# Projection units with the left 256 tokens through all chunks first, then the right 256, in one bank

## The reference

```python
# layer 1: differential attention beside a sparse attention with compressed tokens
x = x + rms_norm(hybrid_mixer(rms_norm(x, ...), ...), attn_post_norm)
x = x + rms_norm((silu(h @ w_gate) * (h @ w_up)) @ w_down, ffn_post_norm)
# layer 2: short convolution beside forgetting attention ("fox"), then SwiGLU
m = shortconv_fox_mixer(u, w_in, b_forget, w_short_conv, w_out)
# layer 3: conformer convolution module (31 taps), then SwiGLU
m = conformer_conv_module(u, w_pw1, b_pw1, w_dw, b_dw, ln_g, ln_b, w_pw2, b_pw2)
```

## Time and profile before

| | |
|---|---|
| time, median of 3 runs | 1901.34 us (1896.58 to 1903.04) |
| the profiled execution | 1899.32 us |
| its span, first to last instruction | 1897.1 us |
| mean granted TensorE clock | 0.991 |
| TensorE busy | 1861.5 us, 98% |
| weight loads busy (beside TensorE) | 1510.6 us, 80% |
| GpSimd busy | 1239.9 us, 65% |
| VectorE busy | 811.3 us, 43% |
| ScalarE busy | 430.2 us, 23% |

### The profile page before, as it was taken

How to read it: one execution, slowest core, us unless ns; L and a number is a source line. 1 busy time by engine, 2 the same in 40 slices (tenths; PEclk the granted TensorE clock), 3 DMA queues, 4 the chain that set the end, 5 groups by cost and what they waited for, 6 DMA issues and landing times.

```text
span 1897.1 us, 25590 instructions
## 1 busy us (share of the span) xinstructions
PE 1861.5 (98%) x9410; PEld 1510.6 (80%) x9410; DVE 811.3 (43%) x1365; ACT 430.2 (23%) x880; POOL 1239.9 (65%) x743
## 2 busy tenths in 40 slices
PE   9999999999999999999999999999999999999997
PEld 7886678888888898777888888889778888888886
DVE  6355755433331144254543333015984453334103
ACT  4336663111110021131311111003334221111000
POOL 7975537866666657664876667557665686666652
PEclk9999999999999999999999999999999999999998
DMA  6431002333333214212233333222323233323311
GB/s 208 132 114 46 12 1 78 110 90 93 95 113 107 79 45 158 83 49 67 89 100 100 88 101 116 100 71 67 100 67 90 78 100 89 99 89 110 106 61 45
DMA packets 44877, 168.27 MB, mean 89 GB/s; under 512 B 4984, under 2 KB 7288, under 8 KB 44672
## 3 DMA queue, kind: packets, MB, share of 16 engines
q1 hardware_dynamic: 44496, 164.56, 27.9%
q10 hardware_dynamic: 304, 2.64, 0.4%
HBM read 165.07 MB, written 2.11 MB: 88 GB/s over the span
## 4 chain that ended last, share of the span: by engine, by line
PE 91%; DVE 4%; POOL 3%; issue 1%; ACT 1%; DMA 0%; POOLq 0%; SPq 0%; DVEq 0%
PE psum L583 27%; PE psum L585 27%; PE psum L584 27%; PE psum L801 2%; POOL w_lo L470 1%; PE psum L785 1%; DVE h_lo L1556 1%; DVE tmp L1598 1%; PE psum L827 1%; POOL w_hi L467 1%; PE psum L633 1%; PE psum L824 1%; PE psum L917 1%; PE psum L931 1%; POOL x L491 1%
## 5 line engine op out<-in xcount | busy, mean ns | idle before, releaser
L470 POOL TENSOR_TENSOR w_lo<-raw,w_hi 128x1024 fp32r<-128x1024 f32 (+1 forms) x286 | 748.4, 2617 | 23.8
L583 PE MATMUL psum<-h_hi,w_hi 128*128 128x512 f32 (+1 forms) x1744 | 663.8, 381 | 13.4 <-POOL w_lo L470 7.4
L584 PE MATMUL psum<-h_lo,w_hi 128*128 128x512 f32 (+1 forms) x1744 | 657.0, 377 | 0.0
L585 PE MATMUL psum<-h_hi,w_lo 128*128 128x512 f32 (+1 forms) x1744 | 657.0, 377 | 0.0
L467 POOL TENSOR_SCALAR w_hi<-raw 128x1024 fp32r<-128x1024 f32 (+1 forms) x286 | 323.7, 1132 | 472.5 <-PE psum L585 446.6
L583 PEld LDWEIGHTS psum<-h_hi,w_hi 128*128 128x128 f32 x1744 | 327.6, 188 | 90.3 <-issue 15.9
L585 PEld LDWEIGHTS psum<-h_hi,w_lo 128*128 128x128 f32 x1744 | 327.2, 188 | 67.7
L584 PEld LDWEIGHTS psum<-h_lo,w_hi 128*128 128x128 f32 x1744 | 327.3, 188 | 66.1 <-issue 0.2
L583 PE MATMUL psum<-g_hi,w_hi 128*128 128x512 f32 (+1 forms) x594 | 219.1, 369 | 0.0
L584 PE MATMUL psum<-g_lo,w_hi 128*128 128x512 f32 (+1 forms) x594 | 218.5, 368 | 0.0
L585 PE MATMUL psum<-g_hi,w_lo 128*128 128x512 f32 (+1 forms) x594 | 218.5, 368 | 0.0
(11 more groups left out here) (282 smaller groups left out, 1876.4 us busy)
## 6 DMA issues: line engine op xcount, KB each, us to landing
raw<-in_wide SPq DMA_DIRECT2D x239, 512.0 KB, 3.6
raw<-in_down SPq DMA_DIRECT2D x48, 704.0 KB, 4.0
decay<-decay_rows ACTq DMA_DIRECT2D x1, 2048.0 KB, 7.8
out<-x SPq DMA_DIRECT2D x16, 128.0 KB, 1.7
x<-in_xt SPq DMA_DIRECT2D x3, 512.0 KB, 6.9
x<-in_xt ACTq DMA_DIRECT2D x1, 512.0 KB, 4.6
angles<-in_angles SPq DMA_DIRECT2D x1, 512.0 KB, 10.4
cols<-in_cols SPq DMA_DIRECT2D x1, 221.0 KB, 4.4
```

The source lines that it names most:

```text
L470: nc.gpsimd.tensor_tensor(w_lo[:, slot, 0:w], raw[:, j % RAW, 0:w], w_hi[:, slot, 0:w].bitcast(F32), ALU.subtract).then_inc(units_split, 1)
L583: pe.matmul(out_ap, lhs[0], rhs[0], start=first, stop=False)
L584: pe.matmul(out_ap, lhs[0], rhs[1], start=False, stop=False)
L585: return pe.matmul(out_ap, lhs[1], rhs[0], start=False, stop=last)
```

## The change

Every unit that went through all its chunks at 512 columns now goes through them twice at 256: chunks 0 to 7 for tokens 0 to 255, then chunks 0 to 7 for tokens 256 to 511, in the same bank. So 24 matmuls of 512 columns become 48 of 256 (33 become 66 in a down unit), each with its own weight load. Only the first matmul of the left half has the start flag. `unit_done` is signalled after the last matmul, as before. Where other work stands between chunks it keeps its place as a share of the unit: what stood behind chunk t stands behind the (2t+2)nd of 16 steps. A wait that nothing used (`k_wait`) is removed. POOL, SP, DVE and ACT have the same instructions in the same order.

```diff
+            def half_of(k, tiles, bank, lhs, rhs, first=True, last=True):
+
+                half, t = slice(k // tiles * H, (k // tiles + 1) * H), k % tiles
+                return three(psum[:, bank, half], lhs, [part[:, half] for part in rhs], first and k == 0, last and t == tiles - 1, skip_group_check=True)
...
-            def feature_unit(h, tiles=UNIT, first=True, last=True, bank=None, width=S, k_wait=None):
+            def feature_unit(h, tiles=UNIT, first=True, last=True, bank=None):
 
                 w = next_unit()
-                for t in range(tiles):
-                    if k_wait is not None:
-                        pe.wait_ge(h_low, k_wait + t + 1)
-                    mm = three(psum[:, bank, 0:width], [w[0](t), w[1](t)], h(t), first and t == 0,
-                               last and t == tiles - 1)
+                for k in range(2 * tiles):
+                    t = k % tiles
+                    mm = half_of(k, tiles, bank, [w[0](t), w[1](t)], h(t), first, last)
                 mm.then_inc(unit_done, 1)
...
-                for t in range(KC):
-                    mm = three(psum[:, bank, :], [unit[0](t), unit[1](t)], h_of(t), t == 0, t == KC - 1)
-                    if t == 2:
+                for k in range(2 * KC):
+                    t = k % KC
+                    mm = half_of(k, KC, bank, [unit[0](t), unit[1](t)], h_of(t))
+                    if k == 5:
                         col_stat()
-                    if t == 5:
+                    if k == 11:
                         row_stat()
...
-                    for t in range(KC):
-                        mm = three(psum[:, woven_bank(first, j), :], [w[0](t), w[1](t)], h_of(t), t == 0, t == KC - 1)
-                        if t == KC - 1:
+                    for k in range(2 * KC):
+                        c, t = k % KC, k // 2
+                        mm = half_of(k, KC, woven_bank(first, j), [w[0](c), w[1](c)], h_of(c))
+                        if k == 2 * KC - 1:
                             mm.then_inc(unit_done, 1)
-                        if t in WEAVE[j]:
+                        if k % 2 and t in WEAVE[j]:
                             fox_round(WOVEN_ROUNDS[j][WEAVE[j].index(t)], first)
```

More of the change, by code:

```diff
@@ L579, in _, with three @@
             n = Count()
[L581 to L585, removed]
+            def three(out_ap, lhs, rhs, first, last, **kw):
+                pe.matmul(out_ap, lhs[0], rhs[0], start=first, stop=False, **kw)
+                pe.matmul(out_ap, lhs[0], rhs[1], start=False, stop=False, **kw)
+                return pe.matmul(out_ap, lhs[1], rhs[0], start=False, stop=last, **kw)
+            def half_of(k, tiles, bank, lhs, rhs, first=True, last=True):
+                half, t = slice(k // tiles * H, (k // tiles + 1) * H), k % tiles
+                return three(psum[:, bank, half], lhs, [part[:, half] for part in rhs], first and k == 0, last and t == tiles - 1, skip_group_check=True)
             def next_unit():
@@ L861, in woven_pairs @@
                     bank, w = free_bank(name), next_unit()
-                    for t in range(KC):
-                        mm = three(psum[:, bank, :], [w[0](t), w[1](t)], h_of(t), t == 0, t == KC - 1)
-                        if t == KC - 1:
+                    for k in range(2 * KC):
+                        c, t = k % KC, k // 2
+                        mm = half_of(k, KC, bank, [w[0](c), w[1](c)], h_of(c))
+                        if k == 2 * KC - 1:
                             mm.then_inc(unit_done, 1)
-                        if t in A_WEAVE[j]:
+                        if k % 2 and t in A_WEAVE[j]:
                             pair_round(A_WOVEN_ROUNDS[j][A_WEAVE[j].index(t)], low_start)
-                        if j == 0 and t in (2, 4):
+                        if k % 2 and j == 0 and t in (2, 4):
                             cmp_turn(t // 4)
@@ L1059, in cmp_turn, with feature @@
                 mm.then_inc(cmp_transposed, 1)
-            def feature(name, k_wait=None):
-                feature_unit(h_of, bank=free_bank(name), k_wait=k_wait)
+            def feature(name):
+                feature_unit(h_of, bank=free_bank(name))
             pe.wait_ge(set_up, 1)
```

## The result

The changed kernel takes 1883.0 us, median of 20 executions, against 1899.8 of the kernel before: ratio 0.9918, with a 95% interval of 0.9905 to 0.9931. So it is 0.8% faster, less than half of what was forecast. What the ratio hides is the spread: the executions of the kernel before lie between 1896.6 and 1903.0 us (one stray left out), those of the changed one between 1872.8 and 1897.5. The one that was profiled first took 1895.97 us.

The account below looks back on a forecast made before the run. TensorE's single stream of matmuls was taken as the bound. 38.8 us gained at the short beat, less 3.0 and 0.5, gave 35.3 off 1899.3: 1864.0, predicted as a 1866 us median, range 1858 to 1917.

Parts of the forecast that it names:

- The beats: TensorE's matmul start distances in the earlier trace: 233.3 ns at 512 columns; 113.3, 117.9 or 120 ns at 256.
- The seams: Between units: nothing gained or lost, as the waits are the same.
- the doubled loop: SwiGLU loop outgrows instruction memory and is fetched at each of 30 passes: +51 us, 1917 with the gain; chance 0.04.
- I take the short beat for the long streams: The three SwiGLU streams: 113.3 ns per 256-column matmul, a pair 6.6 ns less than one of 512.
- the forecast case: Short beat in all three long SwiGLU streams: 1866 us, own range 1860 to 1873; chance 0.50.
- Rival 1: One or two of three SwiGLU streams caught long, 12.9 us each: 1879 or 1892, range 1877 to 1894; chance 0.16.
- the rest of the units: Changed units outside the SwiGLU streams: counted at the same 6.6 ns gain per 512-column matmul as the streams.
- what is cut up and fox_parts: 28 units cut up by other work, half long, 3.0 us back; output units on `fox_parts`, 0.5 us.
- The weight load as the narrow margin: At 256 columns load and matmul are nearly equal, 109 and 113 ns; at 512 the load is hidden twice over.
- Rival 3: The SwiGLU streams get the third value, 120 ns, seen on `fox_parts`: +39.4 us, 1941; chance 0.03.
- a phase between load and matmul: TensorE's 256-column beat looks like a phase between weight load and matmul, caught at the restart; no size given.

Follow-up runs that it names:

- streams_whole: Changed kernel with the loop and down units of the three SwiGLUs put back to 512 columns: 1899.2 us, ratio 0.9999.
- again: The changed kernel run once more without any edit: 12 executions from 1866.5 to 1897.7 us, median 1884.4.
- w288_224: Changed kernel with each unit cut at 288 columns in place of 256, so 288 left and 224 right: 1968.4 us.
- align_halves: Changed kernel with 64 unused bytes per partition ahead of h_hi: 1939.9 us, ratio 1.0222.
- first_wide: Changed kernel with each changed unit's first chunk done over all 512 columns, the other chunks in halves: 1889.7 us, ratio 0.9953.

## Why the prediction was right and wrong

**Right: what bounds, and the prices.** TensorE's stream sets the time, at full clock, and nothing else moved: VectorE, ScalarE and GpSimd have the same busy time to 0.1%. The beats were read rightly from the earlier trace rows: 233, 113 and 118 ns in the loops, and a stream kept its beat over 2942 matmuls. The execution with three short streams took 1866.5 us, where the sum for that case gave 1866, and a stream's difference between long and short was priced at 12.9 us, which puts the levels at 1866, 1879, 1892 and 1905; the profiled executions with none and two long lie at 1866.5 and 1896.0. A long stream measured 346.6 us against 333.5, so 13.1 more. The seams cost nothing (2943 matmuls across all seams of a stream in 346.6 us are 117.8 ns each, as within a unit), and the doubled loop isn't fetched anew (one piece of instructions in 200 us).

**Wrong: "I take the short beat for the long streams."** The prediction had seen that a beat is taken anew at a restart, with two values for the same operands, and then treated the three streams as one draw, "the three have the same code". They are three draws in each execution. Of 32 executions 5 had the time of the forecast case, 19 that of one long stream, 8 that of two. The step that failed is this one: from the tally of short stretches, five of six in `last_unit`, it took the likelier value for all streams in place of counting how many of three would fall the other way. Rival 1, "one or two caught long", got 0.16 and was the case that came. With a chance of about one in three for long (35 of 96 streams in the 32 executions, if the three groups of times are read as none, one and two) the likeliest count is one, and 1879 to 1883 would have been the forecast. Its other support was as thin: the 99-matmul stretches that run on from wide work, short in three of three before, were long in two of three in `streams_whole`. What a single execution showed was luck: the first one profiled took 1896.0 us, the one of `again` 1866.5. The sign was right, the size was twice too large.

**Off in size: the rest of the units.** The sum gave them 1608 x 6.6 = 10.6 us less 3.5 for what is cut up and fox_parts, 7 us. `streams_whole` measured 0 (0.9989 to 1.0009, which is 2 us either way) or, at an equal clock, 3, and the execution with three short streams leaves 32.8 - 3 x 9.5 = 4 us for them. So some 4 of the 17 us that are missing are in this term, and the other 13 are the one long stream. Most of the 4 can be named: ten units of layer 3 have `op_hi` as moving operand, lists them, and the sum gave them the short beat of h. From the second L583 of their last four units to the last one, before and after:

```profile
1425.78 0.39 PE L583 MATMUL psum<-op_hi,w_hi 128*128 128x512 f32 x1
...
1446.78 0.39 PE L583 MATMUL psum<-op_hi,w_hi 128*128 128x512 f32 x1
```

```profile
1430.74 0.28 PE L583 MATMUL psum<-op_hi,w_hi 128*128 128x256 f32 x1
...
1452.88 0.28 PE L583 MATMUL psum<-op_hi,w_hi 128*128 128x256 f32 x1
```

That is 21.00 / 90 = 233.3 ns against 22.14 / 186 = 119.0, so a pair costs 238.1 and the 240 matmuls lose 1.2 us where the sum had them gain 1.6. It is 119.0 in `again` too.

**The weight load as the narrow margin** is borne out in so far as 224 columns don't go below 111.7 ns (`w288_224`). The conclusion from it, that at 512 columns nothing can show, was wrong. A 512-column matmul pays 6.6 ns by its place, in the kernel before too, and that is why halves could win: two of 256 at the short beat cost 226.7 ns, as much as one of 512 at the good place, the shortest beat of 512 columns that ran here. Rival 3 was set aside because the streams don't have the operands of the 120 ns; `align_halves` shows that 64 bytes are enough to give it to them. In the trace each matmul has one load, which starts with the matmul before it and is given 0.19 us at either width: the starts are 0.23 us apart at 512 columns and 0.12 at 256 (PEld at 400 us, before and after). No run shows a load by itself, so that a load takes the 109 ns of the earlier trace rows, and that a matmul has to cover it, is a reading of those rows. That the beat is a phase between load and matmul was a guess, and no run shows it.

**Not settled.** Why a distance of 0 is best for 512 columns and worst for 256, and what in the restart picks the short or the long beat. `first_wide` shows that the beat can be turned over by wide matmuls in a fixed order, so at least there it is a state that is carried on and not chance.

## What to carry to other kernels

Where a trace shows the same matmul at two distances from start to start, at full clock and without a stop, look where its moving operand lies against its stationary one, modulo 256 bytes, before restructuring the loop: 64 bytes of padding gave 1.5% here (1870 us), and at that place halving is a loss (1940 us). Don't judge a change of matmuls to 256 columns, 113 or 118 ns each where 109 was read for a weight load, by one execution: the same program ran from 1866 to 1898 us. Sort the executions by granted clock before reading groups into their times. And where a value is drawn per stream, forecast the count of bad draws, not the best case.

## What was not expected of the hardware

A beat drawn at an idle time of 0.22 us is held for 2942 matmuls, 333.5 or 346.6 us; three wide matmuls between turn it over, unit by unit. A matmul of 224 columns with its own weight load takes 112 ns and not 99. With the distance at a multiple of 256 bytes 512 columns cost 226.7 ns and 256 columns 120; at 192, 233.3 and 113.3 or 117.8.
